# Expert weights in 1024-column blocks, six raw and four split slots, and another place for the gather

## The chip, the cores and the metric

The program runs on one core of one Trainium2 chip. The time is that of one execution on the device, in microseconds (us). Three runs of the kernel before took 1791.83, 1772.27 and 1772.03 us, median 1772.27. One more execution was profiled and took 1767.41 us, with a span of 1765.4 us from the first to the last recorded instruction.

## What is computed

One step of a diffusion backbone in float32: 512 latent and 128 context tokens of width 1024 pass a mixer (a recurrent group and a retention group) and then an expert layer. Only the expert layer bears on the change:

```
def _expert_choice_ffn(h, router_w, wg, wu, wd):
    bsz, n, _ = h.shape
    cap = EC_CAPACITY_FACTOR * n // N_EXPERTS
    probs = jax.nn.softmax((h @ router_w).astype(jnp.float32), axis=-1)
    gate, idx = lax.top_k(jnp.swapaxes(probs, 1, 2), cap)
    b_idx = jnp.arange(bsz)[:, None, None]
    xs = h[b_idx, idx]
    hid = jax.nn.silu(jnp.einsum('becd,edf->becf', xs, wg)) * jnp.einsum('becd,edf->becf', xs, wu)
    ye = jnp.einsum('becf,efd->becd', hid, wd) * gate[..., None].astype(h.dtype)
    return jnp.zeros_like(h).at[b_idx, idx].add(ye)
```

There are 16 experts. Each picks 64 latent and 16 context tokens, 80 rows (slots) together. Its gate and up weights are 1024 x 2048 each and its down weight is 2048 x 1024, so an expert has 24 MB of float32 weights and all of them 384 MB. Both token groups share the weights.

## The kernel before

**Chunks.** Weights come in chunks of 1 MB (128 partitions x 2048 floats), 24 for an expert. SyncE issues the loads into a ring of four raw slots (`load`, L243 and L244 of the profile are its wait and its DMA). ScalarE rounds a chunk to the matmul format (`split_hi`, L250), and VectorE (columns 0 to 1663) and GpSimd (columns 1664 to 2047) subtract that from the raw chunk (`split_lo`, L256). High and low parts go into a ring of three split slots. TensorE multiplies with both parts: x_lo by w_hi, x_hi by w_hi, then x_hi by w_lo, 12 matmuls of 512 columns for a chunk (L899, L900, L904 for gate and up; L914, L915, L918 for down). The high part of a chunk may be made only when TensorE has finished with the chunk that had the slot, which is the third before it (`w_used`), and a raw slot is loaded anew when both low parts are done.

**Blocks.** Gate and up are cut into four blocks of 512 hidden columns, two chunks each, and a load of such a chunk has runs of 512 floats. Down is cut the same way into four blocks of 512 rows. TensorE keeps banks 0 and 1 for gate, 2 and 3 for up, 4 and 5 for down.

**Order.** `body_chunks` writes the order of an expert's body out by hand: u1, d0, g2, u2, d1, g3, u3, d2, then for the next expert g0, then d3, then u0 and g1 of the next, two chunks each. Every engine walks this list with its own small items between the chunks:
- `hid_T` on TensorE (L927) transposes a block of the hidden product; ScalarE (`hidT_hi`, L576) and VectorE (`hidT_lo`, L1348) copy it out of bank 6 in two parts, and down needs both.
- `columns_of` on GpSimd (L1433, L1434) copies the next expert's gate and slot columns, `gather` (L1437) then fetches its 80 token rows from memory with an indirect DMA, `gathered_T` on TensorE (L889) transposes them in two halves, `gathered` on VectorE (L1327, L1331) applies the modulation, `gathered_half` on ScalarE (L565) and `gathered_lo` on VectorE (L1337) split the result. The next expert's g0 needs all of it (`xs_l`).
- `silu` (L572), `hidden` (L1344), and at the end of down `ye` (L607) and the indirect DMA that adds 80 rows to the result in memory (L1466).

On GpSimd the gather stands behind the split of chunk 8 of the body (chunks counted from 0), and TensorE wants it after chunk 9.

**What sets the order.** All engines are in-order; a wait in one's list holds everything behind it. Bodies run in a hardware loop of two, and the last expert stands behind it.

## Time and profile before

| | before |
|---|---|
| median of three runs | 1772.27 us |
| profiled execution | 1767.41 us |
| its span | 1765.4 us |
| first expert matmul, gather for expert 1, gather for expert 15 (start) | 537.3, 579.0, 1619.9 us |
| PE / DVE / ACT / POOL busy | 88 / 70 / 57 / 65% |
| memory traffic in the span | 476.73 MB |

The span has two parts: up to 537 us the modulation, the mixer and the router, and from there to about 1731 us the experts, with a short end behind them. The busy shares of the page mix the two, so the expert part has to be read by itself, and there one body after the other looks nearly the same. A matmul's end is modelled in this profile: matmuls that follow each other overlap in the rows, so the pace is the distance between starts, not the duration. SPq and similar names are an engine's queue of DMA issues. Idle time before a row, and who ended it, stands in brackets.

### The profile page before, as it was taken

The numbers are of one execution on the slowest core, as the hardware profiler recorded it, in microseconds if no ns is written. First come the engines' busy times: TensorE is split into PE (matmuls) and PEld (weight loads), VectorE is DVE, ScalarE is ACT, GpSimd is POOL, SyncE is SP. The second block draws the span as 40 slices with busy tenths as digits, with TensorE's granted clock in tenths as the row PEclk, the third lists the DMA queues.
The fourth block names the chain that finished last, engine by engine and source line by source line (L and its number), as shares of the span: only waits on it lengthen the run. The fifth ranks groups of instructions, "written<-read, shape, count | busy, mean of one in ns | idle before, by whom it ended". The sixth has DMA issues, their size and how long they took to land.

```text
span 1765.4 us, 21080 instructions
## 1 busy us (share of the span) xinstructions
PE 1557.6 (88%) x7025; PEld 1059.3 (60%) x7025; DVE 1235.6 (70%) x1121; ACT 1000.3 (57%) x813; POOL 1155.3 (65%) x517
## 2 busy tenths in 40 slices
PE   5699987888848999999999999999999899999992
PEld 2588765556735556565656656566665565655661
DVE  5525554774565877788787877778878678887773
ACT  6223344243425666676766667667676676766761
POOL 5311231143116797897988989889797797977880
PEclk9699999989858999999999999999999999999996
DMA  9321113256225898999999999999999989989983
GB/s 343 105 72 48 48 49 98 84 174 236 106 107 214 325 357 316 347 348 342 364 344 367 342 339 361 335 377 339 341 376 333 354 329 350 363 330 357 335 317 126
DMA packets 189109, 476.73 MB, mean 270 GB/s; under 512 B 11406, under 2 KB 13706, under 8 KB 172684
## 3 DMA queue, kind: packets, MB, share of 16 engines
q1 hardware_dynamic: 177744, 447.77, 68.8%
q0 software_dynamic: 3728, 13.11, 3.0%
q10 hardware_dynamic: 7596, 15.30, 2.4%
q8 instruction: 26, 0.43, 0.1%
q14 instruction: 15, 0.12, 0.0%
HBM read 462.51 MB, written 13.64 MB: 270 GB/s over the span
## 4 chain that ended last, share of the span: by engine, by line
POOL 41%; issue 22%; PE 20%; DVE 7%; DMA 5%; ACT 4%; POOLq 0%; ACTq 0%; SPq 0%; DVEq 0%
POOL w_lo L256 37%; PE bank L287 3%; PE bank L288 3%; PE bank L286 3%; ACT w_hi L250 2%; POOL arena L1437 2%; DMA raw<-in_ada_w 2%; POOL gate_e L1433 1%; PE bank L852 1%; DVE w_lo L256 1%; PE bank L769 1%; PE bank L692 1%; DMA arena<-xn_rows,slot_e 1%; PE bank L899 1%; PE bank L900 1%
## 5 line engine op out<-in xcount | busy, mean ns | idle before, releaser
L256 POOL TENSOR_TENSOR w_lo<-raw,w_hi 128x384 fp32r<-128x384 f32 (+1 forms) x424 | 1032.1, 2453 | 512.5 <-ACT w_hi L250 507.6
L256 DVE TENSOR_TENSOR w_lo<-raw,w_hi 128x1664 fp32r<-128x1664 f32 (+1 forms) x424 | 902.3, 2139 | 379.0 <-ACT w_hi L250 376.8
L250 ACT CAST w_hi<-raw 128x2048 fp32r<-128x2048 f32 x424 | 806.5, 1910 | 340.8 <-PE bank L904 90.5
L899 PE MATMUL bank<-w_hi,act_lo 128*80 128x512 f32 x1024 | 410.9, 401 | 19.6 <-DVE act_lo L1337 19.5
L900 PE MATMUL bank<-w_hi,act_hi 128*80 128x512 f32 x1024 | 406.5, 397 | 0.0
L904 PE MATMUL bank<-w_lo,act_hi 128*80 128x512 f32 x1024 | 279.4, 394 | 3.9 <-POOL w_lo L256 3.7
L914 PE MATMUL bank<-w_hi,act_lo 128*80 128x512 f32 x512 | 204.3, 399 | 16.9 <-DVE act_lo L1348 13.8
L899 PEld LDWEIGHTS bank<-w_hi,act_lo 128*80 128x80 f32 x1024 | 155.9, 152 | 102.1 <-issue 21.9
L904 PEld LDWEIGHTS bank<-w_lo,act_hi 128*80 128x80 f32 x1024 | 151.8, 149 | 92.1 <-issue 9.8
L900 PEld LDWEIGHTS bank<-w_hi,act_hi 128*80 128x80 f32 x1024 | 153.8, 150 | 79.7 <-issue 2.8
L915 PE MATMUL bank<-w_hi,act_hi 128*80 128x512 f32 x512 | 201.1, 393 | 0.0
L918 PE MATMUL bank<-w_lo,act_hi 128*80 128x512 f32 x512 | 139.9, 395 | 3.2 <-POOL w_lo L256 3.2
L914 PEld LDWEIGHTS bank<-w_hi,act_lo 128*80 128x80 f32 x512 | 75.8, 148 | 69.4 <-issue 15.2
L565 ACT CAST act_hi<-arena 128x320 fp32r<-128x320 f32 x32 | 14.7, 459 | 165.2 <-DVE arena L1331 165.2
L918 PEld LDWEIGHTS bank<-w_lo,act_hi 128*80 128x80 f32 x512 | 75.3, 148 | 47.8 <-DVE w_lo L256 5.4
L915 PEld LDWEIGHTS bank<-w_hi,act_hi 128*80 128x80 f32 x512 | 76.1, 149 | 38.7 <-issue 0.4
L286 PE MATMUL bank<-act_lo,w_hi 128*128 128x512 f32 (+1 forms) x256 | 88.1, 344 | 2.4 <-DVE arena L1063 2.4
L287 PE MATMUL bank<-act_hi,w_lo 128*128 128x512 f32 (+1 forms) x256 | 87.3, 341 | 0.0
L288 PE MATMUL bank<-act_hi,w_hi 128*128 128x512 f32 (+1 forms) x256 | 86.9, 340 | 0.0
L286 PE MATMUL bank<-w_lo,act_hi 128*128 128x512 f32 x160 | 65.6, 410 | 0.0
L288 PE MATMUL bank<-w_hi,act_hi 128*128 128x512 f32 x160 | 63.5, 397 | 0.0
L287 PE MATMUL bank<-w_hi,act_lo 128*128 128x512 f32 x160 | 63.5, 397 | 0.0
(208 smaller groups left out, 1400.9 us busy)
## 6 DMA issues: line engine op xcount, KB each, us to landing
raw<-in_exp_gate SPq DMA_DIRECT2D x128, 1024.0 KB, 5.4
raw<-in_exp_up SPq DMA_DIRECT2D x128, 1024.0 KB, 5.4
raw<-in_exp_down SPq DMA_DIRECT2D x128, 1024.0 KB, 5.8
raw<-in_ada_w SPq DMA_DIRECT2D x24, 1024.0 KB, 6.1
raw<-in_w_in SPq DMA_DIRECT2D x12, 1024.0 KB, 5.2
arena<-in_x_lat ACTq DMA_DIRECT2D x8, 512.0 KB, 9.1
raw<-in_w_out SPq DMA_DIRECT2D x4, 1024.0 KB, 7.5
xn_rows<-arena ACTq DMA_DIRECT2D x5, 512.0 KB, 2.7
```

Of the source, the lines that this page charges most:

```text
L250: nc.scalar.copy(w_hi[:, n % WS, :], raw[:, n % RAW, :]).then_inc(hi_done, 1)
L256: ops.tensor_tensor(w_lo[:, n % WS, at], raw[:, n % RAW, at], w_hi[:, n % WS, at], ALU.subtract).then_inc(done, 1)
L286: nc.tensor.matmul(out, lh, rl, start=start, stop=False, **kw)
L287: nc.tensor.matmul(out, ll, rh, start=False, stop=False, **kw)
L288: return nc.tensor.matmul(out, lh, rh, start=False, stop=stop, **kw)
L899: mm(dst, x[1][:, kk, :], wh[:, k, :], start=(kk == 0), stop=False)
L900: mm(dst, x[0][:, kk, :], wh[:, k, :], start=False, stop=False)
L904: last = mm(dst, x[0][:, kk, :], wl[:, k, :], start=False, stop=(kk == 7))
L914: mm(psum[4 + q][0:SLOTS, :], x[1], wh[:, j, at], start=(b == 0 and half == 0 and j == 0), stop=False)
L915: mm(psum[4 + q][0:SLOTS, :], x[0], wh[:, j, at], start=False, stop=False)
L918: last = mm(psum[4 + q][0:SLOTS, :], x[0], wl[:, j, q * 512:(q + 1) * 512], start=False, stop=(b == 3 and half == 1 and j == 1))
L1437: pool.indirect_dma_start(xg[0:SLOTS, pr2, :], None, xn_rows, bass.IndirectOffsetOnAxis(slot_e[pr2][:, :], 0), bounds_check=TOK - 1).then_ ...
```

## The change

Gate, up and down are now cut into two blocks of 1024 with four chunks each. A chunk of gate or up holds two runs of 1024 floats (4 KB) for each partition instead of four of 512. The order of a body is g1, d0, u1, g0 of the next expert, d1, u0 of the next expert. There are six raw slots for the expert part (two of them in the arena) and four split slots (the fourth lies in `act_hi` and `act_lo`), so a high part waits for the fourth chunk before it. The gather's columns have buffers of their own (`slot_in`) beside those of the scatter (`slot_out`), and the gather moves to the head of a body: its columns are copied behind the split of chunk 4, it is issued behind that of chunk 5, and TensorE wants it after chunk 4. The small items of ScalarE and VectorE get new places. The line numbers move too: L256 becomes L284, L889 L936, L899 L946, L900 L947, L904 L950, L1437 L1484. The loads for the first expert, eight chunks instead of six, stand ahead of the first body.

In the list of GpSimd around the head of a body, w_lo, gate_e and slot_e are its splits and column copies, and f_rows and arena are written by the scatter and the gather. Before:

```order
L1466 DMA f_rows<-arena,slot_e 640x1024
L1469 REGISTER_ALU
L1469 COMPARE_AND_BRANCH
L256 TENSOR_TENSOR w_lo<-raw,w_hi 128x384 [waits hi_done] x4
L256 TENSOR_TENSOR w_lo<-raw,w_hi 128x384 [waits hi_done,gatheredT_ps,f_rows_added]
L1433 COPY gate_e<-gates 80x1
L1434 COPY slot_e<-slots 80x1
L256 TENSOR_TENSOR w_lo<-raw,w_hi 128x384 [waits hi_done,expert_columns]
L1437 DMA arena<-xn_rows,slot_e 80x1024
```

and in the changed kernel:

```order
L1518 DMA f_rows<-arena,slot_out1 640x1024
L1521 REGISTER_ALU
L1521 COMPARE_AND_BRANCH
L284 TENSOR_TENSOR w_lo<-raw,w_hi 128x384 [waits hi_done,gatheredT_ps]
L1480 COPY gate_e<-gates 80x1
L1481 COPY slot_in1<-slots 80x1
L284 TENSOR_TENSOR w_lo<-raw,w_hi 128x384 [waits hi_done,gather_columns]
L1484 DMA arena<-xn_rows,slot_in1 80x1024
```

Between the scatter of one expert and the gather for the next there were six splits; there are two.

In the list of TensorE the gather's transposes now follow the first down chunk of a body (banks 4 and 5):

```order
L950 MATMUL bank4<-w_lo,act_hi 80x512 [waits lo_done_pool,lo_done_dve]
L950 MATMUL bank5<-w_lo,act_hi 80x512
L950 MATMUL bank4<-w_lo,act_hi 80x512
L950 MATMUL bank5<-w_lo,act_hi 80x512
L1011 ISA
L1012 ISA [waits gathered]
L936 MATMUL bank7<-const,arena 128x80 [waits rows_gathered]
L936 MATMUL bank7<-const,arena 128x80 x3
```

The transposes themselves are the same; before, they stood behind the second down block.

On VectorE the second half of the gathered rows is now split behind the low part of chunk 14 (the first row), and the hidden product of u1 follows:

```order
L284 TENSOR_TENSOR w_lo<-arena,w_hi 128x1664 [waits hi_done]
L1381 TENSOR_TENSOR act_lo<-arena,act_hi 128x320 [waits gathered_hi]
L1388 TENSOR_TENSOR arena<-bank,arena 80x512 [waits silu_out,w_used] x2
L284 TENSOR_TENSOR act_lo<-arena,act_hi 128x1664 [waits hi_done]
```

Before, it stood behind the low part of chunk 16, with the modulation of that half right ahead of it; TensorE waited for it ahead of chunk 16, and does so ahead of chunk 12 now.

The diff, cut to its core (the plain renamings and the wording of the matmul helper are left out):

```diff
+RAW_X, WS_X = 6, 4
...
+    raw_more = [region(8192, CH), region(10240, CH)]
+    w_hi_more, w_lo_more = act_hi[:, 3072:3072 + CH], act_lo[:, 3072:3072 + CH]
...
-    def expert_source(e, kind, b, half):
+    def expert_source(e, kind, b, part):
 
         if kind == "d":
-            w = exp_down[bass.ds(e, 1), b * 512:(b + 1) * 512, :].rearrange("o (p j) n -> p (o j) n", p=P)
-            return w[:, 2 * half:2 * half + 2, :]
+            w = exp_down[bass.ds(e, 1), b * 1024:(b + 1) * 1024, :].rearrange("o (h p j) n -> p (o h) j n", p=P, h=2)
+            return w[:, part // 2, 2 * (part % 2):2 * (part % 2) + 2, :]
         w = {"g": exp_gate, "u": exp_up}[kind]
-        w = w[bass.ds(e, 1), :, b * 512:(b + 1) * 512].rearrange("o (k p) n -> p (o k) n", p=P)
-        return w[:, 4 * half:4 * half + 4, :]
+        w = w[bass.ds(e, 1), :, b * 1024:(b + 1) * 1024].rearrange("o (k p) n -> p (o k) n", p=P)
+        return w[:, 2 * part:2 * part + 2, :]
 
     def body_chunks(last):
 
-        order = [("u", 1, 0), ("d", 0, 0), ("g", 2, 0), ("u", 2, 0), ("d", 1, 0), ("g", 3, 0), ("u", 3, 0), ("d", 2, 0)]
-        if not last:
-            order += [("g", 0, 1)]
-        order += [("d", 3, 0)]
-        if not last:
-            order += [("u", 0, 1), ("g", 1, 1)]
-        return [(kind, b, half, nxt) for kind, b, nxt in order for half in range(2)]
-
-    FIRST_CHUNKS = [(kind, b, half) for kind, b in (("g", 0), ("u", 0), ("g", 1)) for half in range(2)]
-
-
-
-    def chunk_view(ring, n, cols):
-        return ring[:, n % ring.shape[1], :].rearrange("p (k n) -> p k n", n=cols)
-
-
-    def load(sp_e, n, e, src, cols):
-        if n >= RAW or not isinstance(e, int):
-            sp_e.wait_ge(lo_pool, e * PER_E + (n - RAW + 1))
-            sp_e.wait_ge(lo_dve, e * PER_E + (n - RAW + 1))
-        sp_e.dma_start(chunk_view(raw, n, cols), src).then_inc(raw_in[n % RAW], 16)
+        order = [("g", 1, 0), ("d", 0, 0), ("u", 1, 0)] + [("g", 0, 1)] * (not last) + [("d", 1, 0)] + [("u", 0, 1)] * (not last)
+        return [(kind, b, part, nxt) for kind, b, nxt in order for part in range(4)]
+
+    FIRST_CHUNKS = [(kind, 0, part) for kind in "gu" for part in range(4)]
...
+        j = n - N_EXP
+        if j < RAW:
+            if n >= RAW:
+                sp_e.wait_ge(lo_pool, n - RAW + 1)
+                sp_e.wait_ge(lo_dve, n - RAW + 1)
+        elif j == RAW:
+            sp_e.wait_ge(xn_out, 16 * TILES)
+            sp_e.wait_ge(h2_ps, 2 * TILES)
+        elif j == RAW + 1:
+            sp_e.wait_ge(sl_rd, 1)
+        else:
+            sp_e.wait_ge(lo_pool, e * PER_E + (n - RAW_X + 1))
+            sp_e.wait_ge(lo_dve, e * PER_E + (n - RAW_X + 1))
...
+            act.wait_ge(w_used, e * PER_E + (n - WS_X + 1))
+        elif n >= WS:
+            act.wait_ge(w_used, n - WS + 1)
+        nc.scalar.copy(w_chunk(w_hi, n), raw_chunk(n)).then_inc(hi_done, 1)
```

ScalarE, the items between the splits:

```diff
+                own = e + nxt
+                if (kind, b) == ("g", 1) and part in (1, 2):
+                    hidT_hi(e, part - 1)
+                if (kind, b) == ("g", 0) and part in (1, 2):
+                    hidT_hi(e, part + 1)
+                if not last or i + WS_X < len(chunks):
+                    split_hi(act, N_BODY + i + WS_X, e)
+                if kind == "d" and b == 0:
+                    if part < 2:
+                        used(act, N_BODY + 3, e)
+                        act.wait_ge(hid_rd, 4 * e + 2)
+                        silu(e, 2 + part)
+                    if part == 2 and not last:
+                        gathered_half(e + 1, 1 - pr2, 0)
+                if not last and (kind, b, part) == ("u", 1, 1):
                     gathered_half(e + 1, 1 - pr2, 1)
-                if not last or i + WS < len(body_chunks(last)):
-                    split_hi(act, N_BODY + i + WS, e)
-                if half and kind == "g":
-                    silu(N_BODY + i, e, b)
-                    if b:
-                        hidT_hi(e + nxt, b - 1)
-                if last and kind == "u" and b == 1 and half:
+                if not last and kind == "d" and b == 1 and part < 2:
+                    used(act, N_BODY + 15, e)
+                    act.wait_ge(hid_rd, 4 * e + 4)
+                    silu(own + 1, part)
```

TensorE, the waits and the items:

```diff
+                if part == 0:
+                    if kind == "g":
+                        pe.wait_ge(sl_ev, 4 * e + (4 if nxt else 2))
+                        if nxt:
+                            pe.wait_ge(xs_l, 2 * e + 4)
+                    elif kind == "u":
+                        pe.wait_ge(hid_rd, 4 * e + (4 if nxt else 2))
+                if kind == "d":
+                    if part % 2 == 0:
+                        pe.wait_ge(ht_lo, 4 * e + (2 * b + part // 2 + 1))
+                    down(n, e, b, part)
                 else:
-                    if half == 0:
-                        pe.wait_ge(ht_lo, 4 * e + (b + 1))
-                    down(n, e, b, half)
-                if half and kind == "g" and b:
-
-                    pe.wait_ge(ht_lo, 4 * own + (b - 1))
-                    hid_T(own, b - 1)
-                    if b == 1:
-                        pe.wait_ge(ye_rd, 2 * e + 2)
-                if not last and half and kind == "d" and b == 1:
+                    up_or_gate(n, e, kind, part, xs[1 - pr2 if nxt else pr2])
+                if kind == "g" and part in (1, 2):
+
+                    half = 2 * (1 - b) + part - 1
+                    if part == 2:
+                        pe.wait_ge(ht_lo, 4 * e + half)
+                    hid_T(e, half)
+                if last and (kind, b, part) == ("u", 1, 3):
+                    hid_T(e, 2)
+                    pe.wait_ge(ht_lo, 4 * e + 3)
+                    hid_T(e, 3)
+                if last and (kind, b, part) == ("d", 1, 1):
+                    pe.wait_ge(gbias2, 16)
+                    pe.wait_ge(sl_ev, 4 * NEXP)
+                    pe.wait_ge(hid_rd, 4 * NEXP)
+                    gate_rows(rows, (0, 1, 2, 3))
+                if not last and (kind, b, part) == ("d", 0, 0):
                     pe.wait_ge(xs_f, 2 * e + 2)
                     pe.wait_ge(xg_in, 16 * e + 32)
                     gathered_T(1 - pr2, 0)
-                if not last and half and kind == "u" and b == 3:
+                if not last and (kind, b, part) == ("d", 0, 3):
                     pe.wait_ge(xs_f, 2 * e + 3)
                     gathered_T(1 - pr2, 1)
-                if half and kind == "d" and b == 2:
-                    pe.wait_ge(ht_lo, 4 * e + 3)
-                    hid_T(e, 3)
-                    if last:
-                        pe.wait_ge(gbias2, 16)
-                        pe.wait_ge(sl_ev, 4 * NEXP)
-                        gate_rows(rows, (0, 1, 2, 3))
+                if not last and (kind, b, part) == ("u", 0, 3):
+                    pe.wait_ge(ye_rd, 2 * e + 2)
```

VectorE:

```diff
-                if not last and (kind, b, half) == ("g", 3, 0):
+            for i, (kind, b, part, nxt) in enumerate(chunks):
+                n = N_BODY + i
+                if (kind, b) == ("g", 1) and part in (1, 2):
+                    hidT_lo(e, part - 1)
+                if (kind, b) == ("g", 0) and part in (1, 2):
+                    hidT_lo(e, part + 1)
+                if kind == "u" and part == 3:
+                    for half in range(2):
+                        hidden(n, e, e + nxt, 2 * b + half)
+                if last and (kind, b, part) == ("u", 1, 3):
+                    hidT_lo(e, 2)
+                    hidT_lo(e, 3)
+                if not last or i + WS_X < len(chunks):
+                    split_lo(dve, "dve", n + WS_X, e)
+                if not last and (kind, b, part) == ("d", 0, 1):
                     gathered(e + 1, 0)
+                if not last and (kind, b, part) == ("d", 0, 3):
                     gathered_lo(e + 1, 1 - pr2, 0)
-                if not last and (kind, b, half) == ("d", 2, 0):
+                if not last and (kind, b, part) == ("u", 1, 0):
                     gathered(e + 1, 1)
+                if not last and (kind, b, part) == ("u", 1, 2):
                     gathered_lo(e + 1, 1 - pr2, 1)
```

GpSimd:

```diff
-                at = (kind, b, half)
-                if not last and at == ("g", 2, 0):
+            for i, (kind, b, part, nxt) in enumerate(chunks):
+                if not last and i == 0:
+
+                    pool.wait_ge(ga_ps, 2 * e + 2)
+                if not last and i == 1:
+                    pool.wait_ge(col_ct, 2 * e + 4)
+                if i == len(chunks) - 3:
 
                     pool.wait_ge(f_add, 16 * e + 16)
-                    pool.wait_ge(ga_ps, 2 * e + 2)
-                if not last and at == ("g", 2, 1):
-                    pool.wait_ge(col_ct, 2 * e + 4)
                 if i == len(chunks) - 1:
+                    pool.wait_ge(sc_ct, e + 1)
                     pool.wait_ge(ye_rd, 2 * e + 2)
-                if not last or i + WS < len(chunks):
-                    split_lo(pool, "pool", N_BODY + i + WS, e)
-                if not last and at == ("g", 2, 0):
+                if not last or i + WS_X < len(chunks):
+                    split_lo(pool, "pool", N_BODY + i + WS_X, e)
+                if not last and i == 0:
                     columns_of(e + 1, 1 - pr2)
-                if not last and at == ("g", 2, 1):
+                if not last and i == 1:
                     gather(1 - pr2)
-            pool.indirect_dma_start(f_rows, bass.IndirectOffsetOnAxis(slot_e[pr2][:, :], 0), ye[0:SLOTS, :], None,
+                if i == len(chunks) - 3:
+                    nc.gpsimd.tensor_copy(slot_out[pr2][:, :], slots[:, bass.ds(e, 1)]).then_inc(sc_ct, 1)
```

## Rows read from the trace of the kernel before

**Rows 1.** Stretches: each engine's busy us, granted clock, DMA share, GB/s.

```profile
1208.40:1262.40 54.00, 53.02 (x240) 34.54 (x239) 43.17 (x28) 37.09 (x26) 46.89 (x23) 1.00 1.03 383
...
600.00:1700.00 1100.00, 1038.90 (x4609) 667.62 (x4608) 868.03 (x619) 744.39 (x533) 939.26 (x413) 0.99 0.95 348
```

**Rows 2.** GpSimd in the first body: the gather for expert 1.

```profile
578.99 2.70 POOL L1437 DMA_INDIRECT arena<-xn_rows,slot_e  x1 [0.15 <-issue]
```

**Rows 3.** The gather's line: all 16, and from issue to landing.

```profile
L1437 POOL DMA_INDIRECT arena<-xn_rows,slot_e x16: 1067/2489/2702, 528.2 to 1619.9; - x16
...
DMA to landing us min/median/max: 4.0/6.5/9.0
```

**Rows 4.** TensorE in a body: start, us, instruction, idle before in brackets.

```profile
1240.88 1.08 PE L904 MATMUL bank<-w_lo,act_hi 128*80 128x512 f32 x4
1241.80 0.59 PE L927 MATMUL bank<-const,arena 80*128 80x80 f32 x4
...
1244.08 1.07 PE L904 MATMUL bank<-w_lo,act_hi 128*80 128x512 f32 x4
...
1249.58 1.09 PE L918 MATMUL bank<-w_lo,act_hi 128*80 128x512 f32 x4
1250.50 0.39 PE L914 MATMUL bank<-w_hi,act_lo 128*80 128x512 f32 x1
...
1252.34 1.09 PE L918 MATMUL bank<-w_lo,act_hi 128*80 128x512 f32 x4
1254.41 0.50 PE L889 MATMUL bank<-const,arena 80*128 80x80 f32 x4 [0.98 <-DMA arena<-xn_rows,slot_e]
...
1275.29 0.46 PE L899 MATMUL bank<-w_hi,act_lo 128*80 128x512 f32 x1 [1.41 <-DVE act_lo L1337]
```

**Rows 5.** TensorE's waits from 600 to 1700 us: total, times, longest.

```profile
PE bank L889 <- DMA arena<-xn_rows,slot_e: 20.8, 14, 4.2
PE bank L899 <- DVE act_lo L1337: 17.2, 15, 1.5
PE bank L914 <- DVE act_lo L1348: 13.1, 25, 0.9
PE bank L904 <- POOL w_lo L256: 3.3, 8, 0.8
```

**Rows 6.** Stretches of three long waits for the gather, and behind each.

```profile
1404.70:1409.70 5.00, 5.00 (x15) 3.22 (x16) 3.88 (x7) 0.93 (x2) 2.71 (x1) 0.50 1.05 423
...
663.50:669.00 5.50, 5.50 (x16) 3.56 (x17) 3.14 (x5) 1.96 (x2) 3.00 (x2) 0.50 0.98 399
1624.40:1628.10 3.70, 0.32 (x2) 0.00 (x0) 3.70 (x3) 2.56 (x2) 1.48 (x2) 1.00 0.94 278
1628.20:1631.60 3.40, 3.40 (x11) 2.32 (x12) 3.40 (x3) 0.38 (x1) 1.01 (x1) 0.51 1.04 401
```

**Rows 7.** TensorE and ScalarE at the end: transposes of the hidden product, copy.

```profile
1719.11 0.59 PE L927 MATMUL bank<-const,arena 80*128 80x80 f32 x4
...
1719.74 0.43 ACT L576 CAST act_hi<-bank 128x320 fp32r<-128x320 f32 x1 [1.19 <-PE bank L927]
```

**Rows 8.** ScalarE in the same body.

```profile
1236.59 1.92 ACT L250 CAST w_hi<-raw 128x2048 fp32r<-128x2048 f32 x1 [0.97 <-PE bank L918]
...
1250.70 1.91 ACT L250 CAST w_hi<-raw 128x2048 fp32r<-128x2048 f32 x1 [0.84 <-PE bank L918]
```

**Rows 9.** VectorE in the same body.

```profile
1238.54 1.89 DVE L256 TENSOR_TENSOR w_lo<-raw,w_hi 128x1664 fp32r<-128x1664 f32 x1 [1.00 <-ACT w_hi L250]
...
1274.57 0.49 DVE L1337 TENSOR_TENSOR act_lo<-arena,act_hi 128x320 fp32r<-128x320 f32 x1 [0.52 <-ACT act_hi L565]
```

**Rows 10.** GpSimd in the same body, up to the gather.

```profile
1238.58 2.73 POOL L256 TENSOR_TENSOR w_lo<-raw,w_hi 128x384 fp32r<-128x384 f32 x1 [0.17 <-ACT w_hi L250]
...
1246.55 1.03 POOL L256 TENSOR_TENSOR w_lo<-raw,w_hi 128x384 fp32r<-128x384 f32 x1 [0.16 <-POOL slot_e L1434]
1247.72 2.50 POOL L1437 DMA_INDIRECT arena<-xn_rows,slot_e  x1
```

More of the change, by code:

```diff
@@ L1371, in body @@
[L1371 to L1382 removed]
+            if last:
+                gate_row(4, (0, 1, 2, 3))
@@ L1444, in _ @@
         gather(0)
[L1445 removed]
+        split_lo(pool, "pool", N_EXP + 3)
+        for n in range(N_EXP + WS_X, N_BODY + WS_X):
             split_lo(pool, "pool", n)
```

181 lines of the change are left out of this document (87 added, 94 removed).

## The prediction

> **What bounds the kernel now.** The page gives one span for two different programs, so I read the expert part alone. First the stretch from 600 to 1700 us [rows 1]: TensorE is busy 1038.9 of 1100 us at a granted clock of 0.99, no other engine reaches 940, and the DMA share is 0.95. TensorE sets the pace and the transfers are close behind. Then the length of a body: the gather for expert 1 starts at 579.0 us [rows 2], the last at 1619.9 [rows 3], with 14 bodies between them, so a body takes 74.35 us. Then what TensorE needs when nothing holds it [rows 4]: a chunk is 2.76 us (1249.58 to 1252.34), one with the hidden product's transposes is 3.20 (1240.88 to 1244.08), so these cost 0.44, and the gather's transposes 0.50. A body is 24 x 2.76 + 4 x 0.44 + 2 x 0.50 = 69.0 us. The remaining 5.3 us are waits and slow stretches. The waits [rows 5] sum to 60.5 us over 14.8 bodies, 4.1 for each: 20.8 for gathered rows, 17.2 for their low part, 13.1 for the hidden product's low part, and 9.4 for late splits (3.3 in the row shown, the rest in two rows of the same kind). The last 1.2 are partly the clock [rows 6]: behind three long waits for the gather TensorE ran 5.0, 5.5 and 3.4 us at a clock of 0.5, the 1.2 GHz level, which loses half of each, 7 us or 0.5 a body.
>
> So the change can give back at most 5.3 us a body, and only where a wait of TensorE gets shorter.
>
> **The change part by part.**
>
> *Longer runs in the loads.* They take no instruction off TensorE. The traffic already ran at 383 GB/s for 54 us [rows 1], which is 1.05 MB in 2.74 us, the pace of a chunk. Priced at nothing, because TensorE covers it; what faster transfers save is in the late splits below. If TensorE needed only its 69.0 us, the transfers would have to keep 383 GB/s, which they did.
>
> *Four split slots, six raw ones.* A high part may be made one chunk earlier, so ScalarE and VectorE can be 2.76 us later without harm. The late splits go: 9.4 / 14.8 = -0.64 us a body. It can't be more than that.
>
> *The hidden product.* Its transposes are now at least a chunk ahead of the down chunks that need the low part, so the wait of 13.1 / 14.8 = -0.88 goes. What is late next is below.
>
> *The gather.* This is the term that decides. I count from the moment when TensorE ends chunk 1 of a body and starts the transposes of the hidden product. They take 0.59 and ScalarE's copy starts 0.04 later and takes 0.43 [rows 7]. In ScalarE's list the high part of chunk 5 follows, 1.92 [rows 8]; it can't be made earlier, since its slot is free only after chunk 1. That is 2.98. GpSimd starts its low part 0.07 later and takes 2.73 while VectorE does its own [rows 9, 10], and 0.14 behind it the gather starts, at 5.92. The trace of before shows the same step, with the transposes behind chunk 5: 1241.80, and the gather at 1247.72 [rows 4, 10], 5.92 too. From there to TensorE's transposes it was 6.69 (1254.41), and landing alone is 6.5 in the median, 4.0 to 9.0 [rows 3]. So the rows are there at 12.6. Before, TensorE asked for them four chunks on, at 11.46 (1252.34 + 0.92), and waited 1.0 to 1.15. Now it asks after chunk 4, three chunks on with two sets of transposes between: 3 x 2.76 + 2 x 0.44 = 9.16. The ordinary wait becomes 3.45, **2.3 us more in each of 15 bodies**. With the late landings the mean goes from 20.8 / 14 = 1.5 to 3.8. The gather also stands two splits behind the scatter on GpSimd's queue instead of six; the scatter's issue is over before the split of chunk 4, whose high part is not ready sooner, so I add nothing. The bounds of this term: if GpSimd gets ahead of VectorE the low part takes 1.03 [rows 10], the gather starts 1.7 sooner, and with a landing of 4.0 the wait is gone (1.5 less than before); with a landing of 9.0 each time it is 5.8 (4.3 more). I take 2.3, because VectorE started 0.04 ahead of GpSimd in the rows and in the new list has nothing else at that point.
>
> *The low part of the gathered rows.* It now stands behind the low part of chunk 14 on VectorE, and that needs TensorE to be through with chunk 10. From the end of chunk 10: ScalarE starts 0.20 later [rows 4, 8], 1.92 for the high part, 0.03 and 1.89 for VectorE's low part, 0.49 for the rows' low part [rows 9], and TensorE goes on 0.23 after that [rows 4]. That is 4.76, and TensorE is there after chunk 11, at 2.76. The wait is 2.0, where it was 17.2 / 15 = 1.15: +0.85. Queued behind this item is the hidden product of u1, which TensorE needs only two chunks on, so nothing else waits. Bounds: nothing (it stays at 1.15) to +1.9 (GpSimd holds VectorE up for one of its splits of 1.03 [rows 10]).
>
> *Column copies.* One more on GpSimd in a body, at its end. GpSimd is idle 160 of 1100 us [rows 1], over 10 us a body, which covers one small copy; nothing, or 2 us a body less of that cover if the copy stands behind one of VectorE's splits (1.89 [rows 9]).
>
> *The clock.* The three long waits for the gather, one of them the 3.7 us up to 1628.1 and the longest 4.2 [rows 5, 6], were each followed by a stretch at 0.5 [rows 6], at a cost of 2.5, 2.75 and 1.7, 2.3 in the mean; a wait of 1.0 as in [rows 4] was not. The new ordinary wait of 3.45 lies next to the first kind. I take 7 bodies of 15 for it, 4 more than now: +9 us; from 0 to 12 more, 0 to +28.
>
> *Both ends.* In the last expert nothing stands between u1 and d1, so product, transposes, copy and low part lie open once, each about half a us, two of them in [rows 7]: about +3, from 0 to 6. At the start more chunks lie ready, but TensorE waits for the router and the first gather there: nothing, to 2 us worse if loads run beside that gather.
>
> **Sum.** 2.3 + 0.85 - 0.88 - 0.64 = +1.63 us a body, 15 times +24.5; clock +9; end +3: +36.5. On the profiled execution's 1767.4 that is 1803.9. Its own median lies 5 us above that execution, and a difference of 2% (35 us) is about what a measurement tells from none. So I forecast **1804 us**, on the edge of slower by 2%.
>
> **The rivals.**
>
> *The gather is in time* (the other side, faster). GpSimd comes first and the landing is near its low end, so the gather no longer ends any wait. It decides once gather and landing together are 3.4 us shorter than in the rows. A body is then 69.0 + 2.0 and 0.8 of unexplained rest, 71.8; 15 x -2.55 = -38, end +3: 1732 us. Against it: the median landing is 6.5 [rows 3], and VectorE is idle when that high part is ready, so it starts first as it did in [rows 9, 10].
>
> *The landing gets 2 us shorter* because fewer packets stand before it. The wait is 1.5, the clock stays up: 24.5 - 30 + 3 - 5 gives 1760.
>
> *The transfers set the pace.* Then the body can't move in either direction and the time stays at 1767 to 1772. For it: share 0.95 over 1100 us. Against it: the 54 us at 383 GB/s. The Trainium skill ("DMA: Bandwidth & Descriptors", section on where 436 GB/s comes from) says that memory gives a core about 358 GB/s and binds loads like these; a body's 25.2 MB would take 70.3 us by that, an estimate from the page. By that rule a kernel with fewer waits could not get below it; the trace disagrees, with 383.
>
> *The clock falls at every wait.* Twelve more slow stretches at 2.3 to 2.75: 24.5 + 30 + 3 gives 1825, and with late landings 1835. For it: three of three.
>
> *Chances.* Forecast 0.43 (1790 to 1815), clock at every wait 0.27, shorter landing 0.13, transfers 0.05, gather in time 0.12. Slower by over 2% is the clock case and a third of the forecast's, 0.42; faster is the gather in time, 0.12; within 2% is 0.46. The range 1745 to 1838 leaves out the gather in time and 0.05 above.
>
> **What would show it.** In the changed kernel's waits, L936 for the rows should have some 55 us in total and be the first, L946 for L1381 some 30, and the waits for the hidden product and for low parts almost none. A body should be 75 to 77 us from gather to gather. In order of time the gather should start 5.9 us after the transposes behind chunk 1. Behind such waits the clock should read 0.5 in some bodies. The forecast is wrong if the gather starts earlier than that, if it lands within 4 us, or if matmuls no longer follow each other at 0.23 us.

## The result, and the profile after it

| | before | after |
|---|---|---|
| median of the runs | 1772.15 us (1767.05 to 1791.83) | 1925.64 us (1910.99 to 1930.27) |
| profiled execution | 1767.41, span 1765.4 | 1921.75, span 1920.0 |
| a body, gather to gather | 74.35 us | 84.30 us |
| last gather to the end | 145.5 us | 160.8 us |

The changed kernel is slower: its time is 1.087 times that of before, 95% interval 1.080 to 1.094. The forecast was 1804, its range 1745 to 1838. The direction was right and the size far too small.

Fourteen bodies took 9.95 us more each, 139 of the 155 us. The stretch of the experts in the changed kernel, to be read beside [rows 1] (its columns), and the gather's line, beside [rows 2, 3]:

```profile
600.00:1850.00 1250.00, 1097.97 (x4663) 703.71 (x4662) 868.32 (x626) 761.51 (x539) 895.66 (x431) 0.93 0.89 308
```

```profile
579.04 2.50 POOL L1484 DMA_INDIRECT arena<-xn_rows,slot_in  x1
```

```profile
L1484 POOL DMA_INDIRECT arena<-xn_rows,slot_in x16: 1076/2496/2503, 530.0 to 1759.2; - x16
...
DMA to landing us min/median/max: 7.7/9.0/9.5
```

Every figure fell: TensorE from 94% busy to 88%, its granted clock from 0.99 to 0.93, the transfers from 348 to 308 GB/s. Nothing runs nearer to its limit, so the time went into waits and into the slower clock. The landing of the gather rose from 6.5 to 9.0 us. A body is (1759.2 - 579.04) / 14 = 84.30 us. TensorE's waits, total, times and longest, beside [rows 5]:

```profile
PE bank L936 <- DMA arena<-xn_rows,slot_in: 93.4, 14, 7.1
PE bank L946 <- DVE act_lo L1381: 48.4, 14, 3.5
PE bank L936 <- DVE arena L1375: 7.0, 14, 0.6
PE bank L946 <- issue: 3.3, 1, 3.3
```

The wait for the hidden product's low part and the waits for late splits have left the list. The wait for rows went from 1.5 to 6.7 us a body, the one for their low part from 1.15 to 3.5, and a small third one is new. Now one body in order of time, each engine apart. TensorE at chunk 1 and at the rows, beside [rows 4]:

```profile
1252.43 0.59 PE L967 MATMUL bank<-const,arena 80*128 80x80 f32 x4
...
1268.51 0.80 PE L936 MATMUL bank<-const,arena 80*128 80x80 f32 x4 [6.72 <-DMA arena<-xn_rows,slot_in]
```

ScalarE's high parts of chunks 4 and 5, VectorE's low part of chunk 5, then GpSimd up to the gather, beside [rows 10], and the load that SyncE issues next to it:

```profile
1249.86 1.91 ACT L278 CAST w_hi<-raw 128x2048 fp32r<-128x2048 f32 x1 [0.86 <-PE bank L950]
...
1253.38 1.92 ACT L278 CAST w_hi<-raw 128x2048 fp32r<-128x2048 f32 x1
```

```profile
1255.33 2.58 DVE L284 TENSOR_TENSOR w_lo<-raw,w_hi 128x1664 fp32r<-128x1664 f32 x1 [1.15 <-ACT w_hi L278]
```

```profile
1252.19 2.92 POOL L1518 DMA_INDIRECT f_rows<-arena,slot_out  x1 [0.15 <-issue]
1254.68 1.48 POOL L284 TENSOR_TENSOR w_lo<-raw,w_hi 128x384 fp32r<-128x384 f32 x1
1255.64 2.30 POOL L1480 COPY gate_e<-gates 80x1 f32 x1
1255.76 2.30 POOL L1481 COPY slot_in<-slots 80x1 uint32 x1
1258.22 1.02 POOL L284 TENSOR_TENSOR w_lo<-raw,w_hi 128x384 fp32r<-128x384 f32 x1 [0.16 <-POOL slot_in L1481]
1259.39 2.50 POOL L1484 DMA_INDIRECT arena<-xn_rows,slot_in  x1 [0.15 <-issue]
```

```profile
1259.27 0.37 SPq L267 DMA_DIRECT2D raw<-in_exp_up  x1
```

The gather starts 6.96 us behind the transposes (1259.39 - 1252.43), where the forecast had 5.92, and the rows are used 9.12 us after that, where it had 6.69. The high part of chunk 5 was ready at 1255.30, as forecast. But GpSimd was behind: the high part of chunk 4 was there at 1251.77, its own low part had to stand behind the scatter's issue of 2.92 us and started at 1254.68, the two column copies, beside VectorE's low part of chunk 5, took until 1258.06, and chunk 5 had its turn at 1258.22. Now VectorE, ScalarE and TensorE where the rows' low part is made, to be read with [rows 8, 9]:

```profile
1198.96 1.31 DVE L1381 TENSOR_TENSOR act_lo<-arena,act_hi 128x320 fp32r<-128x320 f32 x1
1200.20 2.74 DVE L284 TENSOR_TENSOR w_lo<-raw,w_hi 128x1664 fp32r<-128x1664 f32 x1
...
1203.43 0.92 DVE L1375 TENSOR_TENSOR arena<-arena,modc 128x256 f32<-128x256 f32 x2
...
1206.70 1.89 DVE L284 TENSOR_TENSOR w_lo<-arena,w_hi 128x1664 fp32r<-128x1664 f32 x1 [0.54 <-ACT w_hi L278]
1208.51 1.28 DVE L1381 TENSOR_TENSOR act_lo<-arena,act_hi 128x320 fp32r<-128x320 f32 x1
```

```profile
1204.39 0.46 ACT L594 CAST act_hi<-arena 128x320 fp32r<-128x320 f32 x1 [1.54 <-DVE arena L1375]
1204.76 1.91 ACT L278 CAST w_hi<-arena 128x2048 fp32r<-128x2048 f32 x1
```

```profile
1209.92 0.71 PE L946 MATMUL bank<-w_hi,act_lo 128*80 128x512 f32 x1 [3.47 <-DVE act_lo L1381]
```

The same 128x320 subtraction took 0.49 in [rows 9] and 1.28 here, beside a split of GpSimd. Ahead of it, ScalarE waited 1.54 us for the scaled copy of the rows before it could go on to the chunk's high part, and VectorE waited 0.54 for that. Last, the clock behind each of the two waits and between them (columns as in [rows 1]):

```profile
1209.95:1216.70 6.75, 6.75 (x18) 4.02 (x19) 2.83 (x3) 1.34 (x1) 0.70 (x1) 0.55 0.96 303
...
1268.60:1275.00 6.40, 6.40 (x20) 4.09 (x21) 0.00 (x0) 0.68 (x1) 0.00 (x0) 0.58 1.00 400
...
1220.00:1260.00 40.00, 40.00 (x181) 26.19 (x180) 29.34 (x19) 30.11 (x22) 37.65 (x19) 1.00 0.94 324
```

At 0.55 and 0.58 most of both stretches is at the 1.2 GHz level, and 3.0 and 2.7 us of work are lost: 5.7 us in this body.

The account of a mean body: 84.3 is 69.0 of work, 6.7 + 3.5 + 0.5 of waits, and 4.6 left for the clock and a small rest. The bodies aren't alike. Up to the gather at 1430 us all but the first take 85.2 to 85.5 us, and the last three take 81.8 or 81.9, with the same waits. There the clock stays up behind the low part's wait: it reads 1.00 from 1548.80 to 1558.80 us, right behind a wait of 3.46 us, where the ten microseconds from 1209.95 on read 0.70.

### The profile page after: what moved, and what is told of

Read it like the earlier page. It is cut to its first block, busy times and chain, and to the rows that moved or that the text cites. A ratio compares the mean times of both kernels' runs of the same rounds, so it can differ in the third digit from the quotient of the medians.

```text
span 1920.0 us, 21113 instructions
## 1 busy us (share of the span) xinstructions
PE 1607.2 (84%) x7025; PEld 1088.8 (57%) x7025; DVE 1224.7 (64%) x1121; ACT 1007.7 (52%) x813; POOL 1103.8 (57%) x533
## 4 chain that ended last, share of the span: by engine, by line
POOL 34%; issue 26%; PE 23%; DVE 7%; ACT 4%; DMA 4%; POOLq 1%; ACTq 0%; SPq 0%; DVEq 0%
POOL w_lo L284 22%; POOL act_lo L284 7%; PE bank L315 3%; PE bank L314 3%; PE bank L316 3%; PE bank L946 3%; PE bank L947 3%; PE bank L950 3%; ACT w_hi L278 2%; POOL f_rows L1518 2%; POOL gate_e L1480 2%; DMA raw<-in_ada_w 1%; DMA arena<-xn_rows,slot_in 1%; POOL arena L1484 1%; DVE w_lo L284 1%
## 5 line engine op out<-in xcount | busy, mean ns | idle before, releaser
L284 POOL TENSOR_TENSOR w_lo<-raw,w_hi 128x384 fp32r<-128x384 f32 (+1 forms) x232 | 490.9, 2120 | 475.9 <-ACT w_hi L278 470.2
L284 DVE TENSOR_TENSOR w_lo<-raw,w_hi 128x1664 fp32r<-128x1664 f32 (+1 forms) x232 | 469.5, 2024 | 309.2 <-ACT w_hi L278 309.1
L278 ACT CAST w_hi<-raw 128x2048 fp32r<-128x2048 f32 x232 | 443.1, 1911 | 258.1 <-PE bank L950 165.7
L946 PE MATMUL bank<-w_hi,act_lo 128*80 128x512 f32 x1152 | 485.1, 421 | 53.9 <-DVE act_lo L1381 50.6
L947 PE MATMUL bank<-w_hi,act_hi 128*80 128x512 f32 x1152 | 479.3, 416 | 0.0
L284 POOL TENSOR_TENSOR w_lo<-arena,w_hi 128x384 fp32r<-128x384 f32 x96 | 254.8, 2654 | 194.2 <-ACT w_hi L278 193.7
L950 PE MATMUL bank<-w_lo,act_hi 128*80 128x512 f32 x1152 | 329.6, 410 | 0.0
L284 DVE TENSOR_TENSOR w_lo<-arena,w_hi 128x1664 fp32r<-128x1664 f32 x96 | 195.5, 2038 | 207.3 <-ACT w_hi L278 207.3
L278 ACT CAST w_hi<-arena 128x2048 fp32r<-128x2048 f32 x96 | 183.2, 1909 | 190.7 <-PE bank L950 190.7
L946 PEld LDWEIGHTS bank<-w_hi,act_lo 128*80 128x80 f32 x1152 | 185.5, 161 | 162.1 <-issue 79.1
L950 PEld LDWEIGHTS bank<-w_lo,act_hi 128*80 128x80 f32 x1152 | 179.6, 156 | 104.7 <-issue 15.0
L947 PEld LDWEIGHTS bank<-w_hi,act_hi 128*80 128x80 f32 x1152 | 182.8, 159 | 98.7 <-issue 17.8
L284 POOL TENSOR_TENSOR act_lo<-raw,act_hi 128x384 fp32r<-128x384 f32 x64 | 144.5, 2258 | 39.2 <-ACT act_hi L278 38.6
L946 PE MATMUL bank<-act_hi,act_lo 128*80 128x512 f32 x384 | 152.2, 396 | 0.0
L947 PE MATMUL bank<-act_hi 128*80 128x512 f32 x384 | 150.3, 391 | 0.0
L284 DVE TENSOR_TENSOR act_lo<-raw,act_hi 128x1664 fp32r<-128x1664 f32 x64 | 126.8, 1981 | 32.3 <-ACT act_hi L278 32.1
L936 PE MATMUL bank<-const,arena 80*128 80x80 f32 x128 | 20.9, 304 | 119.4 <-DMA arena<-xn_rows,slot_in 110.7
L950 PE MATMUL bank<-act_lo,act_hi 128*80 128x512 f32 x384 | 104.5, 394 | 0.0
L936 PEld LDWEIGHTS bank<-const,arena 80*128 80x128 f32 x128 | 14.6, 181 | 133.9 <-DMA arena<-xn_rows,slot_in 99.2
```

Of the source, the lines that this page charges most:

```text
L278: nc.scalar.copy(w_chunk(w_hi, n), raw_chunk(n)).then_inc(hi_done, 1)
L284: ops.tensor_tensor(w_chunk(w_lo, n)[:, at], raw_chunk(n)[:, at], w_chunk(w_hi, n)[:, at], ALU.subtract).then_inc(done, 1)
L936: last = tr(psum[7][:, k * SLOTS:(k + 1) * SLOTS], xg[0:SLOTS, pr2, at], ident[0:SLOTS, 0:SLOTS])
L946: mm(dst, x[j][1], wh[:, j, at], start=(first and j == 0), stop=False)
L947: mm(dst, x[j][0], wh[:, j, at], start=False, stop=False)
L950: last = mm(psum[banks + q][0:SLOTS, :], x[j][0], wl[:, j, at], start=False, stop=(final and j == 1))
```

## The experiments

Kernels are compared with the one before, as a ratio with its 95% interval. Unless said otherwise each is an edit of the changed kernel. Two questions: which terms make the 10 us a body, and why the rows land so late (landing is the time from the issue of a transfer to the arrival of its data). For the second there were three theories at first: A, the scatter just ahead on GpSimd; B, the number of loads that six raw slots leave outstanding; P, the longer runs of the loads.

**e1, the gather a body ahead.** GpSimd issues it behind its split of chunk 19 for the expert after next. The copy of its slot column goes with it, and two gathers now stand ahead of the first body.

```diff
+                if ahead and i == 14:
+                    slots_of(e + 2, pr2)
+                if ahead and i == 15:
+                    gather(pr2)
...
-                if not last and i == 1:
-                    gather(1 - pr2)
```

> The changed kernel with the gather for expert e+2 issued behind the split of chunk 19 of body e, almost a body before TensorE wants it. My theory, that the excess is the gather's late start at the head of a body plus what follows from it: the wait for gathered rows (93.4 us in the changed kernel) goes to zero, and the clock keeps its full level there; what is left is the wait for the rows' low part, 3.5 us a body or less. A body falls from 84.3 us to 73 to 77, the time to 1755 to 1815 us. Rival, that the new block shape or the transfers set the pace: TensorE then waits for splits or loads instead, a body stays over 81 us and the time over 1870.

Measured: 1799.4 us, ratio 1.018 (1.012 to 1.024). Its TensorE waits:

```profile
PE bank L946 <- DVE act_lo L1381: 48.5, 14, 3.5
PE bank L936 <- DVE arena L1375: 19.9, 14, 1.5
```

The wait for rows is gone, and with it 126 us, more than the 93.4 that stood in the waits, although the wait for the scaled copy grew from 7.0 to 19.9. The rest fits the clock behind the long wait, which e4 tests. A body takes 75.9 us. What is left is above all the low part of the rows, untouched at 48.5.

**e2, no scatter** but in the last expert, so 15 experts' results aren't added.

```diff
-            pool.indirect_dma_start(f_rows, ..., compute_op=ALU.add).then_inc(f_add, 16)
+            if last:
+                pool.indirect_dma_start(f_rows, ..., compute_op=ALU.add).then_inc(f_add, 16)
```

> The changed kernel without the indirect DMA that adds an expert's rows to the result, except for the last expert, so 15 experts' results are left out. Theory A, that the scatter just ahead of the gather on GpSimd's queue delays it: the gather starts 5.9 us after the transposes behind chunk 1 instead of 6.9, and the landing falls from 9.1 to 6.7 us, so the wait falls from 6.7 to 3.4 us and the time by 50 us or more (with the clock up, by 80). Theory B, that the landing is slow because more loads stand before the gather's packets: only the start moves by 1 us, the landing stays at 8.5 to 9.2, the time falls by 10 to 25 us.

Measured: 1892.0 us, ratio 1.069 (1.061 to 1.077). The wait for rows and the landing:

```profile
PE bank L936 <- DMA arena<-xn_rows,slot_in: 71.0, 14, 5.9
```

```profile
DMA to landing us min/median/max: 7.5/8.5/9.3
```

The time is 34 us less, between what the two theories gave. The wait falls by 1.6 us a body. The larger part is the earlier start: the gather begins 5.84 us behind the transposes (1231.39 - 1225.55 in one body), as the forecast had it, and not 6.96. The landing falls by only 0.5. Theory A explains the start, not the landing. With the scatter out of the way the two column copies take 0.18 us each in the median, where in the changed kernel they take 2.3, and the gather's issue 1.02 instead of 2.50. GpSimd then begins both ahead of VectorE's next split, where in the rows above it begins them behind it.

**e3, four raw slots** as before, so that fewer loads are outstanding.

```diff
-RAW_X, WS_X = 6, 4
+RAW_X, WS_X = 4, 4
```

> The changed kernel with four raw slots instead of six, so at most four loads are outstanding as before; the split slots stay at four. Theory B (outstanding loads delay the gather's packets): the landing falls from 9.1 to 6.5 to 7.5 us, the gather's wait from 6.7 to 4 to 5 us, the time by 25 to 70 us unless loads come late. Theory A (the scatter, or the 4 KB packets themselves): the landing stays at 8.5 or more and the time within 10 us.

Measured: 1942.7 us, ratio 1.098 (1.088 to 1.108). The landing:

```profile
DMA to landing us min/median/max: 4.0/8.8/10.1
```

It did not get shorter, as theory B needs it. The count of slots is not what sets it. The time is 17 us above the changed kernel's, where either theory had expected less; the intervals overlap.

**e4, TensorE kept busy in the wait** by nine matmuls into a bank that nobody reads.

```diff
+                    for _ in range(9):
+                        mm(psum[7][:, 0:C_N], ident, const[:, :], start=True, stop=True)
                     pe.wait_ge(xg_in, 16 * e + 32)
```

> The changed kernel with nine float32 matmuls of 426 columns, whose result nobody reads, on TensorE ahead of its wait for the gathered rows. They should fill about 6 us of the 6.7 us wait. If the clock's fall behind the wait costs what the sum says, the granted clock stays at 1.0 behind the gather, 2.5 to 5 us a body come back and the time falls by 30 to 75 us although TensorE has more to do. If the slow stretches cost nothing, because something else is late anyway, the time stays within 10 us or rises.

Measured: 1885.9 us, ratio 1.067 (1.061 to 1.073), 40 us less than the changed kernel, though the rows come no sooner (landing 9.2 in the median). The wait is now filled:

```profile
PE bank L936 <- DMA arena<-xn_rows,slot_in: 4.7, 10, 0.9
```

So about 40 us, 2.8 a body, is what the clock loses because TensorE stands idle here. Not all of it lies behind this one wait: behind the low part's wait the ten microseconds from 1184.80 on read 0.83, where the changed kernel had 0.70, so filling the first wait also shortened the slow stretch behind the second.

**e5, 2 KB runs.** The gate and up loads as two halves of 512 columns.

```diff
+            for q in range(2):
+                sp_e.dma_start(halves(raw_chunk(n))[:, q], src[q]).then_inc(raw_x_in[j % RAW_X], 16)
```

> The changed kernel, but each chunk of gate and up is loaded as two halves of 512 columns, so its runs in memory are 2 KB again; blocks, order, slots and the gather's place stay. Theory P, that the longer runs of the loads delay the gather's packets: the landing falls from 9.1 to 6.5 to 7.2 us, the wait for the rows from 6.7 to about 4.5 us, and the time by 35 to 60 us, to 1865 to 1890 us. Theory O, that run length has no part in it: the landing stays at 8.5 or more, the time stays within 10 us of 1925.

Measured: 1923.3 us, ratio 1.081 (1.073 to 1.089). The landing stays:

```profile
DMA to landing us min/median/max: 7.3/8.9/9.5
```

Theory P falls, and the longer runs bring nothing that can be measured.

**e6, e1 with the rows' transposes behind chunks 0 and 4**, and VectorE's and ScalarE's steps moved with them.

```diff
-                if not last and (kind, b, part) == ("d", 0, 0):
+                if not last and (kind, b, part) == ("g", 1, 0):
                     pe.wait_ge(xs_f, 2 * e + 2)
                     pe.wait_ge(xg_in, 16 * e + 32)
                     gathered_T(1 - pr2, 0)
-                if not last and (kind, b, part) == ("d", 0, 3):
+                if not last and (kind, b, part) == ("d", 0, 0):
                     pe.wait_ge(xs_f, 2 * e + 3)
```

> The changed kernel with the gather almost a body ahead, and with the transposes, the modulation and the splits of the gathered rows three to four chunks earlier in the body (transposes behind chunks 0 and 4, low parts behind chunks 5 and 9). My theory, that TensorE's need sets the pace once its waits are gone: a body takes 69.0 us and up to 1.5 of rest, the clock stays up, the time is 1700 to 1745 us, faster than both kernels. Rival: with less idle time VectorE and GpSimd, which delay each other, or the transfers set the pace; then a body stays at 74 us or more and the time at 1770 or more.

Measured: 1741.2 us, ratio 0.981 (0.976 to 0.986). The first that beats the kernel before, by 1.9%. Its waits:

```profile
PE bank L936 <- DVE arena L1375: 25.8, 14, 1.9
PE bank L946 <- DVE act_lo L1381: 11.0, 14, 0.8
```

A body takes 72.2 us, more than the 70.5 that I had allowed, because these two waits, 2.6 us a body, were left; the time lies within the expected range, near its upper end.

**e7, the same with 2 KB runs.** The edits of e6 and e5 together.

> The same kernel as the one with the rows early, but with 2 KB runs for gate and up, each chunk in two loads. If longer runs are worth something by themselves where nothing waits for a gather, this one is slower than the other by 10 us or more, with ScalarE waiting for loads. If TensorE covers the transfers, as the prediction says, the two are within 8 us.

Measured: 1738.5 us, ratio 0.979 (0.973 to 0.985). The same as e6 within what can be told, where the transfers run at 351 GB/s in both, at a DMA share of 0.98 and 0.99 (600 to 1700 us).

**e8, the low part of the rows first** on VectorE, ahead of its low part of the chunk.

```diff
+                if not last and (kind, b, part) == ("u", 1, 2):
+                    gathered_lo(e + 1, 1 - pr2, 1)
                 if not last or i + WS_X < len(chunks):
                     split_lo(dve, "dve", n + WS_X, e)
```

> The changed kernel with one item moved on VectorE: the low part of the second half of the gathered rows stands ahead of the low part of chunk 14 instead of behind it. My theory, that the 3.5 us wait is this split of 1.9 us and what it does to GpSimd's lock-step with VectorE: the wait falls to 0 to 1.6 us a body, the clock no longer falls there, and the time falls by 30 to 75 us. Rival, that the wait comes from ScalarE's high part or TensorE's own lateness: it falls by less than 0.5 us and the time by less than 10 us.

Measured: 1843.2 us, ratio 1.038 (1.032 to 1.044), 82 us less, more than expected. Its VectorE rows at that place, and its waits:

```profile
1161.92 0.48 DVE L1381 TENSOR_TENSOR act_lo<-arena,act_hi 128x320 fp32r<-128x320 f32 x1
```

```profile
PE bank L936 <- DMA arena<-xn_rows,slot_in: 95.0, 14, 7.3
...
PE bank L946 <- ACT w_hi L278: 3.2, 13, 0.2
```

The wait of 48.4 is gone, and 34 us more; that this is the clock behind it is the reading that fits, the same kind of cost that e4 priced at the other wait. One line's place on one queue was worth 82 us. The subtraction takes 0.48 again: GpSimd is idle beside it, its next split begins at 1162.58.

**e9 and e10, loads held back around the gather.** The landing was still open. Theory C: the gather's packets compete with the loads issued behind it. Theory Q: they wait behind the loads outstanding when it is issued. SyncE waits for the landed rows before the load of chunk 11 (e9), or of chunk 9 (e10).

```diff
+            if held:
+                sp_e.wait_ge(xg_in, 16 * e + 32)
...
+                load(sync, ..., not last and i == 11)
```

> The changed kernel, where SyncE issues the load of a body's chunk 11 (and so all later ones) only when the next expert's rows have landed; chunk 11 is the first load that can be issued once GpSimd has reached the gather. Nothing is left out. Theory C (the gather's packets compete with the loads that are issued behind it): from the gather's start to the transposes it is 6.6 us or less instead of 9.1. Theory Q (they wait behind the loads that were outstanding when it was issued, 1.9 MB): the time stays at 8.5 to 9.5 us. In both the transfers stand idle for a while behind the gather, so the time may be 1880 to 2000 us; what is read is the time to the transposes.

> The same with the hold two chunks sooner: the loads of chunks 9 and 10 are also held until the rows have landed, so that some 1 MB fewer are outstanding when the gather is issued. Theory Q: the time from the gather's start to the transposes falls to 5.5 to 7 us; and by theory C it is as in the kernel with one held load, whatever that shows. If neither changes it (9 us in both), the loads have no part in it. The loads that come late cost the body time of their own: 1900 to 2100 us.

Measured: e9 1877.0 us, ratio 1.058 (1.052 to 1.064); e10 1897.6, ratio 1.069 (1.063 to 1.076). The landing and the first wait of e9, then of e10:

```profile
DMA to landing us min/median/max: 6.0/6.4/7.5
...
PE bank L939 <- DMA arena<-xn_rows,slot_in: 58.1, 14, 5.0
```

```profile
DMA to landing us min/median/max: 5.3/5.4/7.5
...
PE bank L939 <- DVE arena L1378: 46.2, 15, 4.4
PE bank L939 <- DMA arena<-xn_rows,slot_in: 43.1, 14, 3.2
```

Theory C holds: without the loads from chunk 11 on, the first of which is issued 0.12 us ahead of the gather in the rows above, the landing is 6.4 instead of 9.0. Theory Q holds for a smaller part: with the loads ahead held too it is 5.4. No load is in flight then, for from 1246.52 to 1252.00 us, around one of these gathers, the transfers move 60 GB/s, which is the gather's own 0.33 MB. So 5.4 us is this gather's landing when nothing runs beside it. Although e9 leaves the transfers idle for a while behind every gather, it is 49 us faster than the changed kernel, because TensorE waits 35 us less for rows and the clock is down for less time (granted 0.94 from 600 to 1700 us, the changed kernel 0.92). In e10 the loads come late, ScalarE waits 108 us for them, and beside e9 the wait for the scaled copy grows by 40 us while the one for rows falls by 15; it is still 28 us faster than the changed kernel. Both times lie 2 to 3 us under the expected ranges. In e2 to e5, where no load is held back, the landing stayed at 8.5 to 9.2, and in e1 and e6 it was 7.9 and 8.1.

**e11, e6 with both of VectorE's passes over the rows ahead of its split** of the same chunk.

```diff
-                if not last or i + WS_X < len(chunks):
-                    split_lo(dve, "dve", n + WS_X, e)
                 if not last and (kind, b, part) == ("g", 1, 2):
                     gathered(e + 1, 0)
...
                     gathered_lo(e + 1, 1 - pr2, 1)
+                if not last or i + WS_X < len(chunks):
+                    split_lo(dve, "dve", n + WS_X, e)
```

> The kernel whose gather is issued a body ahead with the rows' transposes behind chunks 0 and 4 (1741 us), and VectorE's two passes over the gathered rows (the scaled copy and the low part, for both halves) now ahead of its low part of the same chunk instead of behind it. Nothing is left out. There TensorE still waited 1.8 us a body for the scaled copy before the second transposes and 0.8 us for the low part. Expected: these 2.6 us a body fall to under 1, and with the clock behind them the time is 1690 to 1730 us. Rival: the low part of the chunk, now late by one pass (1.3 us) at four places a body, holds back TensorE or the loads as long: 1735 to 1760 us.

Measured: **1704.4 us** (1699.5 to 1705.9), ratio 0.960 (0.955 to 0.964): 4% faster than the kernel before. A stretch of its experts, its waits, and its gathers:

```profile
600.00:1600.00 1000.00, 995.81 (x4497) 648.33 (x4496) 957.31 (x604) 736.70 (x518) 836.96 (x417) 1.00 1.00 372
```

```profile
PE bank L967 <- DVE act_lo L1392: 5.0, 13, 1.0
PE bank L967 <- DVE arena L1388: 1.8, 1, 1.8
```

```profile
692.53 2.51 POOL L1487 DMA_INDIRECT arena<-xn_rows,slot_in  x1 [0.15 <-issue]
...
1525.38 2.50 POOL L1487 DMA_INDIRECT arena<-xn_rows,slot_in  x1 [0.15 <-issue]
```

TensorE is busy 99.6% of 1000 us at full clock, and a body takes (1525.38 - 692.53) / 12 = 69.4 us, against the 69.0 that the prediction worked out for a TensorE that nothing holds. The landing is 9.7 us in the median here and costs nothing, since nobody waits for it. The blocks of 1024 columns and the slots are those of the changed kernel, so its loss lay in the place of the gather and of a few small items alone.

## Why the prediction was wrong

The forecast body was 76.6 us, clock included; it took 84.3. The steps one by one:

*The floor of 69.0 us*: right, by e11 (69.4).

*The hidden product (-0.88) and the late splits (-0.64)*: right. Neither is left among the waits.

*The gather (+2.3)*: the step that failed first. The wait is 6.7 us a body, not 3.8. Two of its inputs were off. The start: 6.96 for 5.92. I had priced the scatter's nearness at nothing because its issue would be over before the high part of chunk 4 was ready; the issue began 0.42 us after that, took 2.92 (in the kernel before a scatter's issue took 1.45 in the median), and pushed the split of chunk 4 back by 2.9. The two column copies, which I had at nothing as well, then fell beside VectorE's split of chunk 5 and were done only 2.4 us after they began. They don't cost that by themselves: in e2, without the scatter, they take 0.18 each and the gather starts at 5.84. That the trace of before showed "the same step", 5.92, was chance. There the high part of chunk 8 did not stand behind the copy of the transposes, and the time was filled by a copy of a column that took 1.85 us beside VectorE's split, and a split of 1.03. That copy was the warning, and my sum didn't have it. The landing, up to the use of the rows: 9.12 for 6.69. I took the median of before as a property of the gather, though my own rows gave 4.0 to 9.0 and the upper bound had it at 9.0 each time, at 5.8 of wait; even that bound was exceeded because both errors fell together. e9 and e10 show that the landing depends on which loads are issued around it, and the change moves the gather to another place among them.

*The low part of the rows (+0.85)*: mechanism right, size wrong. 3.5 us, not 2.0, and just above the bound of 3.05 (1.15 + 1.9). Of the 1.5 us missing, 0.8 is the subtraction itself (1.28 for 0.49), and the rest ScalarE's late high part, which waited for VectorE's scaled copy: a wait of a helper that the sum did not have. The Trainium skill ("SBUF — State Buffer", section on who interferes with whom) says that a VectorE instruction with two inputs in SBUF contends with a GpSimd instruction that reads SBUF, over a port pair that only one of them holds at a time. The trace agrees: 1.28 to 1.31 beside a split of GpSimd, 0.48 in e8 where none stands there.

*A third wait*, for the scaled copy before the second transposes: 0.5 us a body, not foreseen.

*The clock (+9)*: as large a miss as the gather's. I let it fall in 7 bodies of 15 at 2.3 us, behind one wait. It fell behind the wait for rows in all 15, and behind the low part's wait in the first 11; 4.6 us a body with the small rest, where the forecast had 1.8. e4 prices the first at 2.8 us a body, e8 the second at some 2.4 ((82 - 48.4) / 14). The two can't be added: they would be 5.2, more than the 4.6 there is, and e4 has shown that filling the first wait also shortens the slow stretch behind the second. I had given the clock no price behind the low part's wait at all. Nor does the length of a wait alone decide: of the 15 waits for the low part, 3.3 to 3.5 us each, the last four were not followed by a slow stretch, and in the trace of before a wait of 0.95 us for rows (up to 1108.71) was. From 1109 to 1113 us the clock read 0.57 there; TensorE had stood idle for 0.87 and 0.63 us shortly ahead of it. My "three of three" had left out this fourth case. What decides is not settled by these runs.

Per body that is 2.9 + 1.5 + 0.5 + 2.8 = 7.7 us, 108 over 14 bodies, of the 118 that the forecast was short. The other 10 all lie behind the last gather, for the first starts at 579.0 us in both kernels: from the last gather to the end it is 15.3 us more, where the forecast had about 5. TensorE's waits in that stretch are 13.8 us against 6.1. Its first part is the fifteenth wait of each kind, with the same misses as above; the hidden product that lies open in the last expert waits 2.8 us, and for that +3 was right.

Of the rivals, the one in which the clock falls at every wait had the right mechanism and still only 1825 to 1835, because it stood on the same waits. The rival that transfers set the pace is refuted: e11 moved 372 GB/s for 1000 us with TensorE at 99.6%. The rule weighed in the prediction gave 358 GB/s as a core's share; the Trainium skill ("Perfetto Trace Analysis", Roofline) adds that a core that runs alone can draw more, up to some 120% of it, and the trace agrees, with 104%. Longer runs, priced at nothing, are worth nothing (e7 to e6: 3 us, inside both intervals).

**What stays open.** Before the change a load was also issued with the gather, and the landing was 6.5; which difference in the loads' timing makes it 9.0 is not settled beyond e9 and e10. e3 has as few raw slots as before and lands at 8.8, so it isn't their number. The 6.5 was itself two cases: of the last 14 gathers of the kernel before, 11 landed after 6.3 to 6.7 us and three after 8.1, 8.6 and 9.0, and these three are the long waits of [rows 6]. What was issued and not yet moved when the gather began, counted from the packets in the traces, was 1.55 to 1.62 MB in the 11, 1.66 to 1.97 in the three, 1.84 to 2.13 in the changed kernel, 1.0 in e9 and nothing in e10. But e1 and e6 have 1.6 and land at 7.9 and 8.1, so this amount alone does not decide either.

## What to carry to other kernels

The landing time of a small transfer is not its own: it depends on what is issued around it, so a step that moves it among large loads must be priced with the whole range of landings, or the transfer be issued so early that nobody waits for it. A wait on TensorE can cost more than its length, here 40 to 70% more on the mean, in slow clock behind it, and every wait of a body needs that price, not only the longest. Before blaming the big parts of a change look at the place of its smallest items on each queue: a 0.5 us subtraction behind instead of ahead of a 1.9 us one was worth 82 us of 1925.

## What the runs showed that I had not expected

- One indirect gather of 80 rows: 5.4 us to landing with no load in flight beside it, 6.4 with only those behind it held back, 9.0 with none held.
- GpSimd's two copies of 80x1 held its queue for 2.4 us together (1255.64 to 1258.06), as long as a whole split, where they fell beside a split of VectorE; where none ran they took 0.18 us each (e2). The gather's issue took 2.50 us in the one case and 1.02 in the other.
- The same wait of 3.5 us was followed by a slow clock in 11 bodies and not in the last four, and the bodies without it are 3.5 us shorter (81.8 for 85.3).
- Holding loads back, with the transfers idle for a while in each body, made the kernel 49 us faster (e9).
